# Hybrid two-layer model on one core: the attention's projections in another order, with the compress network and the first two steps' scores among them

## What is computed

```
q, k_c, v_c, k_s, v_s, k_w, v_w, gates = split_cols(h @ w_in, NSA_SPLITS)
def compress(t, pos, w1, w2):                       # 63 blocks of 32 tokens, stride 16
    blk = t.reshape(bsz, seq, G, Dh)[:, cmp_idx] + pos[:, None, :]
    return jax.nn.silu(blk @ w1) @ w2
k_cmp, v_cmp = compress(k_c, ...), compress(v_c, ...)
# per block of queries:
s_c = q_blk @ k_cmp - slopes * dist_c ; p_c = masked_softmax(s_c) ; o_c = p_c @ v_cmp
imp = (sum of p_c over heads) @ cover ; top = top_k(imp, 6)      # forced: first, current, previous block
o_s = attention over the chosen blocks of k_s, v_s
o_w = attention over the last 512 tokens of k_w, v_w
o = g_0 * o_c + g_1 * o_s + g_2 * o_w ;  return o @ w_out
```

## Time and profile before

| What | Value |
|---|---|
| median of three runs | 3088.87 us |
| the profiled execution: its own time | 3087.6 us |
| its span | 3085.9 us |
| PE busy (matmuls) | 2914.6 us (94%) |
| POOL, DVE, ACT busy | 1407.6, 1226.9, 954.9 us |
| end of unit 13, first PE work behind it | 1623.59 us of the span |
| start of the loop's first transposes | 1698.76 us |
| last scores of the loop | 2237.3 us |

### The profile page before, as it was taken

One profiled execution on the slowest core, in us unless ns is written; L12 is line 12 of the kernel. 1 busy time (PEld: TensorE's weight loads), 2 busy tenths in 40 slices (PEclk: granted clock), 3 DMA queues, 4 the chain that ended last, 5 costly groups with the idle time before them and its releaser, 6 DMA issues. The chain is left out here.

```text
span 3085.9 us, 43401 instructions
## 1 busy us (share of the span) xinstructions
PE 2914.6 (94%) x17327; PEld 2343.1 (76%) x17327; DVE 1226.9 (40%) x2021; ACT 954.9 (31%) x1626; POOL 1407.6 (46%) x920
## 2 busy tenths in 40 slices
PE   6998999989999999999995888889999999999998
PEld 4887878877888888888784666555687888888887
DVE  5455463524331331332202677745514331331334
ACT  3444441322330110121101555777713320210211
POOL 2444434656444444444630555545536444444442
PEclk9998999989999999999997999999999999999999
DMA  4100011021111111111114000000011111111111
GB/s 141 47 23 2 15 35 48 15 89 41 48 50 52 48 45 50 48 45 53 42 34 126 2 1 1 1 1 1 15 35 42 48 48 49 51 46 52 48 44 72
DMA packets 212558, 127.57 MB, mean 41 GB/s; under 512 B 9016, under 2 KB 208189, under 8 KB 212285
## 3 DMA queue, kind: packets, MB, share of 16 engines
q1 hardware_dynamic: 210797, 125.32, 13.8%
q10 hardware_dynamic: 1616, 0.21, 0.0%
HBM read 112.94 MB, written 8.39 MB: 39 GB/s over the span
## 5 line engine op out<-in xcount | busy, mean ns | idle before, releaser
L486 POOL TENSOR_TENSOR WH<-WR,ONES 128x1024 fp32r<-128x1024 f32 (+1 forms) x192 | 452.2, 2355 | 1138.4 <-PE PS L1847 964.1
L1847 PE MATMUL PS<-YH,WH 128*128 128x512 f32 x1904 | 590.0, 391 | 5.3 <-POOL WL L489 4.1
L1847 PE MATMUL PS<-YH,WL 128*128 128x512 f32 x1904 | 587.2, 390 | 0.0
L1847 PE MATMUL PS<-YL,WH 128*128 128x512 f32 x1904 | 587.2, 390 | 0.0
L489 POOL TENSOR_TENSOR WL<-WR,WH 128x1024 fp32r<-128x1024 f32 (+1 forms) x192 | 456.0, 2375 | 15.1
L1612 DVE SCALAR_TENSOR_TENSOR X<-PS,PTF,X 128x1023 f32<-128x1023 f32 (+1 forms) x176 | 225.7, 1282 | 562.3 <-ACT X L1090 549.5
L1847 PEld LDWEIGHTS PS<-YH,WH 128*128 128x128 f32 x1904 | 357.3, 188 | 82.3 <-POOL WL L489 4.5
L1847 PEld LDWEIGHTS PS<-YH,WL 128*128 128x128 f32 x1904 | 357.9, 188 | 74.8
L1847 PEld LDWEIGHTS PS<-YL,WH 128*128 128x128 f32 x1904 | 358.0, 188 | 74.6
L1090 ACT ACTIVATE X<-PS,PTF 128x1024 f32<-128x1024 f32 x88 | 106.2, 1207 | 830.3 <-PE PS L1847 823.8
L716 POOL TENSOR_SCALAR X<-X,STAT,SM 128x640 f32<-128x640 f32 (+6 forms) x215 | 176.5, 831 | 163.8 <-DVE STAT L1767 163.7
(11 more groups left out here) (404 smaller groups left out, 3942.7 us busy)
## 6 DMA issues: line engine op xcount, KB each, us to landing
WR<-in_ffn_w_up_dram SPq DMA_DIRECT2D x88, 512.0 KB, 3.8
WR<-in_hy_w_in_dram SPq DMA_DIRECT2D x28, 512.0 KB, 3.8
WR<-in_ffn_w_down_dram SPq DMA_DIRECT2D x32, 448.0 KB, 3.5
WR<-in_ffn_w_down_dram SPq DMA_DIRECT2D x16, 512.0 KB, 3.7
WR<-in_nsa_w_in_dram SPq DMA_DIRECT2D x14, 512.0 KB, 3.7
X<-in_x_dram SPq DMA_DIRECT2D x8, 512.0 KB, 7.2
xt_scratch<-H SPq DMA_DIRECT2D x1, 4096.0 KB, 13.3
WR<-in_hy_w_out_dram SPq DMA_DIRECT2D x8, 512.0 KB, 3.7
```

What stands on the lines that cost most here:

```text
L486: pool.tensor_tensor(WH[:, slot, 0:k, :], WR[:, slot, 0:k, :], ONES[:, :].unsqueeze(1).broadcast_to([P, k, P]), ALU.mult).then_inc(w_hi, 1)
L1847: ins = pe.matmul(PS[:, 2 * slot + a, :], w[:, slot, i, :], y[:, i, a * HALF:(a + 1) * HALF], start=(i == 0 and w is WH and y is hi), stop ...
```

## The change

- The projections' order: k_c and v_c first, then k_s, k_w, v_s, v_w, then the queries (`NSA`).
- The gates' columns follow units 0 and 1, then the compress network's 64 matmuls with the gates' turn after the first 16; its second product follows unit 2, the turning of v_s and v_w unit 6.
- `W1`, `KV2` and `BLK` lie in tiles of `X` that are free at that time, so their loads and copies don't wait for the projections' end. SP's queue: four units' weights, `W1` and second weights, copies of k_c and v_c, two units' weights, copies of k_s and k_w, eight units' weights.
- Unit 13 is written out by tiles; the scores of steps 0 and 1 stand before its third and seventh tile, in banks 4 to 7 (`score_ps`).
- In every later step of the loop the wait for DVE is made per head: the first head's scores need the step before's first head read, the second head's both.
- DVE's six tables are spread over steps 5 to 21, the importance over three steps per group (29, 33, 35 and 61, 62, 63) instead of one; POOL's distances for the selected keys move to steps 64 and 66. The ranking of the first group starts at step 37 (before: 33).

```diff
+        NSA = (8, 9, 10, 12, 11, 13) + tuple(range(MT))
+        W1 = [XF[:, k * SEQ:(k + 4) * SEQ].rearrange("p (l n) -> p l n", l=16) for k in (0, 10)]
+        KV2 = [X[:, 4 + 2 * i:6 + 2 * i, :] for i in range(2)]
+        BLK = [XF[:, (14 + 2 * i) * SEQ:(14 + 2 * i) * SEQ + 16 * NG * NC].rearrange("p (l g n) -> p l g n", l=16, g=NG)
...
+        GROWS = X[0:48, 18, :]
+        H1_BANK = (5, 6, 7, 4)
+        EARLY = 2
...
-        first_select = [group_done + 2, len(steps) - 2]
-        select_at = {first_select[g] + 1 + (2, 1)[g] * i: (g * TT // 2 + i // 3, i % 3) for g in range(NG) for i in range(3 * TT // 2)}
+        rank_at = [group_done - 1 + i for i in (0, 4, 6)], [len(steps) - 4 + i for i in range(3)]
+        select_at = {rank_at[g][2] + (2, 1)[g] * (i + 1): (g * TT // 2 + i // 3, i % 3) for g in range(NG) for i in range(3 * TT // 2)}
...
-            columns(U_NSA, nsa_w, 0, 14)
...
-            sp.wait_ge(psum_free, U_NSA + 14)
+            def nsa_columns(u0, u1):
+                for u in range(u0, u1):
+                    load(U_NSA + u, u % 2, nsa_w[:, :, NSA[u] * P:(NSA[u] + 1) * P])
+
...
-            for dst, src in ((KS2, 10), (KW2, 12)):
-                for g, part in enumerate((lower, upper)):
-                    for half in (lower, upper):
-                        sp.dma_start(X[half, dst[g], :], X[part, src, :]).then_inc(k2_loaded, 16)
-
-            sp.wait_ge(gp_ready, 2)
-            for i in range(2):
-                for g, part in enumerate((lower, upper)):
-                    sp.dma_start(KV2[i][lower, g, :], X[part, 8 + i, :]).then_inc(k2_loaded, 16)
-                    sp.dma_start(KV2[i][upper, g, 0:SEQ - 1], X[part, 8 + i, 1:SEQ]).then_inc(k2_loaded, 16)
+            nsa_columns(0, 4)
+            sp.wait_ge(gemm_done, U_NSA)
             for i, w1 in enumerate((cmp_w1_k, cmp_w1_v)):
                 sp.dma_start(W1[i], w1[0].rearrange("(l p) n -> p l n", p=P)).then_inc(w1_loaded, 16)
...
+            sp.wait_ge(psum_free, U_NSA + 2)
+            for i in range(2):
+                for g, part in enumerate((lower, upper)):
+                    sp.dma_start(KV2[i][lower, g, :], X[part, 8 + i, :]).then_inc(kv2_loaded, 16)
+                    sp.dma_start(KV2[i][upper, g, 0:SEQ - 1], X[part, 8 + i, 1:SEQ]).then_inc(kv2_loaded, 16)
+            nsa_columns(4, 6)
+            sp.wait_ge(h1_ready, 4)
+            for dst, src, u in ((KS2, 10, 2), (KW2, 12, 3)):
+                sp.wait_ge(psum_free, U_NSA + u + 1)
+                for g, part in enumerate((lower, upper)):
+                    for half in (lower, upper):
+                        sp.dma_start(X[half, dst[g], :], X[part, src, :]).then_inc(k2_loaded, 16)
+            nsa_columns(6, 14)
...
-            splits(U_NSA + 2, 12)
-
+            splits(U_NSA + 2, 2)
...
+            pool.wait_ge(gate_e, 1)
...
-            pool.wait_ge(h1_ready, 4)
...
+            splits(U_NSA + 4, 10)
...
+            def compressed_bias():
+                pool.wait_ge(gemm_done, U_NSA + 14)
...
+            compressed_bias()
             for p in range(len(steps)):
+                if p == 2:
+                    block_places()
+                if p in (64, 66):
+                    selected_distances((p - 64) // 2)
...
+                act.activation(X[:, t, 0:HALF], gemm_ps(n % 2)[:, 0:HALF], ACT.Copy, scale=QSC[:, t:t + 1] if t < MT else 1.0).then_inc(n_half, 1)
+
+            nsa_unit(0)
+            nsa_unit(1)
             act.wait_ge(gt_ready, 2)
-            act.activation(Z[0:48, 0, :], PSF[0:48, 6 * HALF:8 * HALF], ACT.Copy).then_inc(gt_sb, 1)
+            act.activation(GROWS, PSF[0:48, 6 * HALF:8 * HALF], ACT.Copy).then_inc(gt_sb, 1)
+            act.wait_ge(gp_ready, 2)
+            act.activation(GATE, PS[:, 4, 0:TT * 48].rearrange("p (c n) -> p c n", c=TT), ACT.Exp, scale=-1.0).then_inc(gate_e, 1)
+            act.wait_ge(kv2_loaded, 16 * 8)
+            for i in range(4):
+                act.wait_ge(h1_ready, i + 1)
+                act.activation(H1[:, i, :], PS[:, H1_BANK[i], 0:NG * NC], ACT.Silu).then_inc(h1_sb, 1)
+            for u in range(2, 7):
+                nsa_unit(u)
...
+                act.activation(X[:, t, :], ps_pair(i), ACT.Copy).then_inc(v_sb, 1)
+            for u in range(7, 13):
+                nsa_unit(u)
...
+            nsa_unit(13)
...
+
+            nsa_unit(0)
+            nsa_unit(1)
+            dve.wait_ge(kv2_loaded, 16 * 8)
             for i in range(2):
...
+            dve.wait_ge(gate_e, 1)
+            link(dve.tensor_scalar(GATE, GATE, 1.0, None, ALU.add))
+            dve.reciprocal(GATE, GATE).then_inc(gate_ready, 1)
+            nsa_unit(2)
             dve.wait_ge(kv_ready, 1)
...
-            dve.wait_ge(ndc_ready, 3)
-
-            link(dve.tensor_scalar(MUL, VI, -1.0, None, ALU.is_lt))
-            link(dve.tensor_scalar(ADD, VI, -1.0, 1e9, ALU.is_ge, ALU.mult))
...
+            for u in range(3, 13):
+                nsa_unit(u)
+
+            def block_rules(part):
+                if part == 0:
+                    dve.wait_ge(ndc_ready, 4)
+                    link(dve.tensor_scalar(MUL, VI, -1.0, None, ALU.is_lt))
...
+                dve.wait_ge(ndc_ready, 1)
...
-            def importance(g):
+            def importance(g, part):
                 v = IMP[:, g * TT:(g + 1) * TT, :]
...
+                if part == 0:
+                    dve.wait_ge(imp_c, (g + 1) * TT)
...
+                elif part == 1:
...
+                else:
...
-            for p in range(AHEAD):
+            dve.wait_ge(k2_loaded, 16 * 8)
+            for p in range(EARLY):
                 bias_step(p)
-            for p in range(AHEAD - 1):
+            for p in range(EARLY):
                 norm_step(p)
+            nsa_unit(13)
+            for p in range(EARLY, AHEAD):
+                bias_step(p)
...
-                    if p in first_select:
-                        importance(first_select.index(p))
+                    for g in range(NG):
+                        if p in rank_at[g]:
+                            importance(g, rank_at[g].index(p))
...
+                    if p % 4 == 1 and 1 <= p // 4 <= 5:
+                        block_rules(p // 4 - 1)
...
-            for u in range(2, 14):
-                unit(U_NSA + u, u % 2, MT, YH, YL)
             pe.wait_ge(gw_split, 2)
             gate_columns(48)
-            for i, t in enumerate((VS, VW)):
-                pe.wait_ge(psum_free, U_NSA + 14)
...
-            gate_turn(48, Z[:, 0, :], 2)
...
+
+            def block_products(i, f):
+                for l in range(16):
...
+            pe.wait_ge(w1_loaded, 16 * 5)
+            pe.wait_ge(blk_ready, 2)
+            block_products(0, 0)
+            gate_turn(48, GROWS, 2)
+            block_products(0, 1)
+            pe.wait_ge(blk_ready, 4)
+            block_products(1, 0)
+            pe.wait_ge(gate_e, 1)
+            block_products(1, 1)
+            unit(U_NSA + 2, 0, MT, YH, YL)
...
+            for u in range(3, 7):
+                unit(U_NSA + u, u % 2, MT, YH, YL)
+            pe.wait_ge(kv_sb, 2)
+            pe.wait_ge(psum_free, U_NSA + 6)
+            for i, t in enumerate((VS, VW)):
+                for tt in range(TT):
+                    ins = pe.transpose(ps_pair(i)[:, chunk(tt)], X[:, t, chunk(tt)], IDENT[:, :])
+                ins.then_inc(v_t, 1)
+            for u in range(7, 13):
+                unit(U_NSA + u, u % 2, MT, YH, YL)
...
-                if p >= 1:
+                if b == 2:
                     pe.wait_ge(neg_ready, 2 * p)
-                if b == 2:
...
                     for i in range(2):
+                        if p >= 1 and a == 0:
+                            pe.wait_ge(neg_ready, 2 * p - 1 + i)
                         part = head_part(h + i)
-                        ins = pe.matmul(gemm_ps(i)[:, a:e], X[part, h // 2, chunk(qt)], X[part, kt, first * P + a:first * P + e],
+                        ins = pe.matmul(score_ps(p, i)[:, a:e], X[part, h // 2, chunk(qt)], X[part, kt, first * P + a:first * P + e],
                                         start=True, stop=True)
...
-            pe.wait_ge(kv_sb, 2)
-            for p in range(AHEAD):
+            pe.wait_ge(v_sb, 2)
+            pe.wait_ge(k2_loaded, 16 * 8)
+            pe.wait_ge(w_split, U_NSA + 14)
+            pe.wait_ge(psum_free, U_NSA + 12)
+            for i in range(MT):
+                if i in (2, 6):
+                    scores((2, 6).index(i))
+                for w, y in ((WH, YH), (WH, YL), (WL, YH)):
+                    for a in range(2):
+                        ins = pe.matmul(PS[:, 2 + a, :], w[:, 1, i, :], y[:, i, tok_half(a)],
+                                        start=(i == 0 and w is WH and y is YH), stop=(i == MT - 1 and w is WL))
+            ins.then_inc(gemm_done, 1)
+            pe.wait_ge(psum_free, U_NSA + 14)
+            for p in range(EARLY, AHEAD):
                 scores(p)
```

129 lines of the change are left out of this document (57 added, 72 removed).

## The result

| | before | changed |
|---|---|---|
| median, us | 3089.18 (3087.88 to 3094.94, 4 runs) | 3056.66 (3055.87 to 3057.41, 4 runs) |
| profiled execution, us | 3087.6 | 3056.54 |
| its span, us | 3085.9 | 3054.8 |
| its mean granted clock | 0.979 | 0.985 |

The ratio is 0.9892, with a 95% interval from 0.9879 to 0.9905: 1.1% faster, 32.5 us by the medians. The forecast was 3051 us, with a range from 3038 to 3066.

The account below looks back on a forecast made before the run. It took PE, 94% busy, as the bound, with waits for weights before the loop and for DVE in it. Passage -30 and loop -7 us took 3087.6 to 3050.6, or 3051 as median; range 3038 to 3066.

Parts of the forecast that it names:

- Steps 1, 2 and 3 of the passage: Between the first two units and the loop's first transposes: gates' columns 11.1 us, PE idle 5.3, the network's 64 products 17.3.
- Steps 5 and 6: End of the passage: scores of steps 0 and 1 inside unit 13, 2.6 us; then waiting for unit 13's result, 1.8.
- Step 7: Last part of the passage: step 2's scores, DVE's bias on them and step 3's scores, 4.4 us to the first transposes.
- one more us: Right behind the passage: the first ten transposes at full clock, 1.3 us instead of 2.49, making the passage -30 us.
- The queues that were moved past: Work passed over on SP's, POOL's and ACT's queues: weights stay hidden and waits hold only later work, all at nothing.
- The importance, -7: In the loop: cutting the importance into three pieces removes most of 9 us of stalls, -7 us, bounds 0 and -9.
- The wait per head, -2: In the loop: only the first head's scores start earlier, -2 us, bounds 0 and -26, apart from the heads' parting.
- The loop, -7 in all: Sum for the loop: importance -7, six tables +2 and wait per head -2 us.
- +2 on the tables: In the loop: six tables spread over five steps of a busy DVE cost +2 us, bounds 0 and +8.
- The loop gives nothing: Rival: DVE's pieces land on steps without slack, ranking still stalls PE, tables take the importance's gain; 3059 us, chance 0.25.
- The two heads fall out of step: Rival: the wait between a step's two score matmuls parts them, about 0.65 us a step, 84 in all; 3135, chance 0.03.
- Late weights: Rival: weights of units 6 to 13 come 4 to 5 us late per unit, eating the 30 us; 3085, chance 0.04.

Follow-up runs that it names:

- unit2_first: Changed kernel with projection unit 2 put ahead of the compress network and unit 3 between its two products: 3046.53 us, ratio 0.9864 to the kernel before.
- scores_behind: Changed kernel with steps 0 and 1's scores behind unit 13's last product instead of inside the unit: 3059.72 us, ratio 0.9887 to the kernel before.
- one_piece: Changed kernel with each group's importance again in one piece and the selection at its old steps: 3071.93 us, ratio 0.9927 to the kernel before.
- select_fine: `unit2_first` with only step 2's second head waiting for unit 13's banks, and group 0's selection cut to one operation a step: 3036.38 us.
- before_head_wait: Kernel before with only the wait per head in place of the wait per step: 3091.08 us, ratio 1.0002 to the kernel before.

## Why the prediction was right, and where its terms were off

The sign, the size and the range held; of the 5.7 us between 3051 and the median, 2 are in the passage and 4 in the loop. 3056.66 lies just above the band from 3046 to 3056 that had the chance of 0.52, and the loop's part came near by errors that cancel in part, as below.

- **Steps 1, 2 and 3 of the passage** held: gates 11.1 us, wait 5.53 (5.3 said), network 10.98 + 5.83 = 16.8 (17.3). The mechanism was as put: copies of 11.4 us behind unit 1's result, then two of DVE's four additions. When `unit2_first` filled the wait, it was worth more than its 5.5 us, 7.6 us with its clock. I had the wait as a cost of the change and did not ask whether the order left a unit to fill it.
- **Steps 5 and 6** held: 1.64 us of waiting, 1.8 said. The scores inside unit 13 are worth 4.7 us by the profile of `scores_behind`, 2.4 by its median.
- **Step 7 and the "one more us"** failed. I let the clock be full by the first transposes, since 5.07 us of waiting had gone. The waits of 1.64 and 1.03 us were followed by half clock too: step 3's scores took 3.24 us, not 1.3, and the transposes still 2.49. It is 178.1 us to the transposes, 176.9 said, and the 1 us in them did not come: -27.7 and not -30.
- **The queues that were moved past** cost nothing, as said: no unit waits for POOL more than before (4.1 us for the whole group in both pages).
- **The importance, -7**, is right in its mechanism and at its own places: 7 us at the first group and 3 at the second, as the 9 us of stalls said. By medians it is -9.5 alone (6.5 to 14.5) and -14.6 taken out of the changed kernel; by the loops -2.1 and -10.4. So the -7 is rather small, but what the cut is worth in a whole loop isn't settled, and the selection's move by four steps is in it.
- **The wait per head, -2**, is 0: the second head ends where the pair ended.
- **The loop, -7 in all**, measured -3.2 by the profiles. The sum of its terms was wrong in kind. I priced each stall at its own place and half clock, and left out that everything behind it then meets the clock at other times: 6.0 us were lost between steps 41 and 61, with 24 us of half clock for 10 and no more waiting than before. With the passage's part, the tables and the wait, but the importance in one piece, the loop is 7.2 us longer, with 20 us more of half clock; the cut gave 10.4, and -3.2 is left. I had put +2 on the tables: no run takes them apart, but up to step 33 the loop is 1.0 us behind in the changed kernel and 1.9 in `one_piece`, so they are at most about that.

**The rivals.** "The loop gives nothing" (3059) was nearer the median than the forecast, by 2.3 against 5.7 us. One of its reasons, that the tables take what the importance frees, is wrong: 1 us against 10. The other, that the ranking pieces of 2 us stall PE as before, is right (11.6 us of waits there against 12.6), and it is part of what `select_fine` takes away. "The two heads fall out of step" did happen where DVE is late, in narrow pairs and in wide ones: the two matmuls of a pair stand 0.74 us apart, a pair of 384 keys takes 1.52 us for 0.92, and the scores' busy time rises by 19.5 us (155.1 to 174.6) with the wait alone. Scores over 1.6 us were to be a sign that the forecast is wrong; step 3's took 3.24 us in the changed kernel, and 2.09 at full clock in `unit2_first`. The sign misled. To the 3 us that `before_head_wait` can tell, the parting costs nothing, since the same time leaves the idle column. The Trainium skill (TensorE: Matmul & The Clock Gate, section Packing small matmuls) says that matmuls are never reordered and that tiles in other rows overlap, each starting a few ns behind the last. The rows agree: a second matmul that waits starts later by its wait, and the overlap goes. The time from one compressed scores to the next, 14.41 us both ways, says that it is free where PE stood still before. "Late weights" did not happen.
